# A two-layer encoder on one core: exponentials ordered behind a copy, five unread products, and one subtraction ahead of the masks

## The reference

```python
for l in range(DEPTH):
    h = _rmsnorm(x, attn_norm_w[l])
    (g_qkv, g_z, g_b, g_a, d_q, d_k, d_v, c_q, c_k, c_v, gate_raw) = _split_cols(h @ w_in[l])
    y_a = _gdn_mixer(g_qkv, g_z, g_b, g_a, ...)      # gated delta rule, both directions
    y_b = _diff_mixer(d_q, d_k, d_v, ...)            # differential attention, 4 heads
    y_c = _gqa_mixer(c_q, c_k, c_v, ...)             # grouped-query attention, 8 heads
    merged = (gates[:, :, 0] * (y_a @ w_branch_a[l]) + gates[:, :, 1] * (y_b @ w_branch_b[l])
              + gates[:, :, 2] * (y_c @ w_branch_c[l]))
    x = x + merged @ w_out[l]
    x = x + _hier_moe(_rmsnorm(x, ffn_norm_w[l]), ...)   # 32 experts, top 2 within the top group
return _rmsnorm(x, final_norm_w)
```

## Time and profile before

| | |
|---|---|
| median of 3 runs | 1574.89 us |
| the runs | 1576.79, 1574.89, 1573.20 us |
| the profiled execution | 1572.78 us |
| its span, first to last instruction | 1570.5 us |
| mean granted clock of TensorE | 0.94 of full speed |
| busy: PE, PEld, DVE, ACT, POOL | 1288.2, 998.3, 681.1, 445.7, 121.0 us |
| DMA | 491 MB, mean 313 GB/s |

### The profile page before, as it was taken

How to read it: one execution, slowest core, us unless ns; L and a number is a source line. 1 busy time by engine, 2 the same in 40 slices (tenths; PEclk the granted TensorE clock), 3 DMA queues, 4 the chain that set the end, 5 groups by cost and what they waited for, 6 DMA issues and landing times. The chain is left out here.

```text
span 1570.5 us, 42304 instructions
## 1 busy us (share of the span) xinstructions
PE 1288.2 (82%) x17356; PEld 998.3 (64%) x17357; DVE 681.1 (43%) x1682; ACT 445.7 (28%) x902; POOL 121.0 (8%) x110
## 2 busy tenths in 40 slices
PE   7998899998886667668799988999898867666665
PEld 6787687776655455446578876787666645445443
DVE  6667856663221221122286777666522321121222
ACT  4456645551000000000145565554400000000000
POOL 2002630000000000000020044200000000000000
PEclk9999999999998988889899999999999988888988
DMA  9521425599999999999974122446999999999996
GB/s 345 203 78 54 135 103 184 212 387 413 424 426 426 427 428 427 428 427 427 410 258 161 55 83 98 174 166 259 387 385 411 426 427 426 428 428 428 427 427 286
DMA packets 81207, 491.05 MB, mean 313 GB/s; under 512 B 13374, under 2 KB 15958, under 8 KB 53718
## 3 DMA queue, kind: packets, MB, share of 16 engines
q1 hardware_dynamic: 81110, 489.68, 76.9%
HBM read 488.61 MB, written 1.05 MB: 312 GB/s over the span
## 5 line engine op out<-in xcount | busy, mean ns | idle before, releaser
L2111 PE MATMUL ps<-ring,arena 128*32 128x128 f32 x5504 | 207.7, 311 | 122.5 <-DMA ring<-in_expert_w_gate_dram 78.4
L2111 PEld LDWEIGHTS ps<-ring,arena 128*32 128x32 f32 x5504 | 179.0, 125 | 161.9 <-DMA ring<-in_expert_w_gate_dram 80.1
L2210 ACT ACTIVATE arena<-ps 128x128 f32<-128x128 f32 x66 | 18.3, 277 | 498.2 <-PE ps L2111 498.2
L2111 PE MATMUL ps<-arena 128*32 128x128 f32 x2688 | 103.9, 313 | 60.0 <-DMA arena<-in_expert_w_gate_dram 42.7
L2316 DVE COPY arena<-ps 128x256 f32<-128x256 f32 x68 | 28.9, 425 | 276.0 <-PE ps L2077 275.9
L2111 PEld LDWEIGHTS ps<-arena 128*32 128x32 f32 x2688 | 89.2, 127 | 79.9 <-DMA arena<-in_expert_w_gate_dram 49.0
L506 POOL TENSOR_TENSOR small<-small,cst 128x8 f32<-128x8 f32 (+1 forms) x21 | 27.7, 1317 | 1193.4 <-DVE small L782 444.5
L1849 DVE TENSOR_TENSOR w_low<-ring,w_high 128x512 fp32r<-128x512 f32 x126 | 85.8, 706 | 52.0 <-ACT w_high L1773 52.0
L2138 PE MATMUL ps<-ring,arena 128*32 128x256 f32 x1376 | 88.7, 389 | 20.7 <-DMA ring<-in_expert_w_down_dram 19.6
L2375 DVE TENSOR_TENSOR arena<-ps,arena 128x128 f32<-128x128 f32 x66 | 25.0, 379 | 181.5 <-ACT arena L2210 181.5
L2212 ACT ACTIVATE arena<-ps 128x256 f32<-128x256 f32 x66 | 25.3, 383 | 275.3 <-PE ps L2138 275.3
(11 more groups left out here) (375 smaller groups left out, 2416.7 us busy)
## 6 DMA issues: line engine op xcount, KB each, us to landing
ring<-in_expert_w_up_dram SPq DMA_DIRECT2D x42, 2048.0 KB, 40.6
ring<-in_expert_w_gate_dram SPq DMA_DIRECT2D x42, 2048.0 KB, 40.4
ring<-in_w_in_dram SPq DMA_DIRECT2D x28, 2048.0 KB, 8.6
ring<-in_expert_w_down_dram SPq DMA_DIRECT2D x44, 1024.0 KB, 39.4
ring<-in_expert_w_down_dram SPq DMA_DIRECT2D x20, 2048.0 KB, 41.9
arena<-in_expert_w_up_dram SPq DMA_DIRECT2D x20, 2048.0 KB, 41.6
arena<-in_expert_w_gate_dram SPq DMA_DIRECT2D x20, 2048.0 KB, 40.3
arena<-in_expert_w_down_dram SPq DMA_DIRECT2D x20, 2048.0 KB, 42.0
```

Source lines behind the costliest of these rows:

```text
L2111: ins = pe.matmul(bank_b[32 * g:32 * g + 32, u * P:(u + 1) * P], xg[:, c], spare[u][:, c, g] if from_spare else w[:, u, c, g], start=(c == ...
```

## The change

```diff
@@ PE, attention block
                 for s in range(STEPS):
                     if s == STEPS - 1:
                         decay_sums()
+                        for n in range(2):
+                            pe.matmul(ps[1][:, :], ident, dv[:, n], start=True, stop=True)
                     if s < LATE:
@@ ACT, attention block
                         act.activation(probsT[:, f % 2].rearrange("p k q -> p (k q)"), ps[4][:, :], ACT.Copy).then_inc(c_pT, 1)
+                        if m == 0 and 4 <= s < STEPS - 1:
+                            exps(s + 1)
                         if s == LATE and m == 0:
                             silu(2)
                     if s >= LATE:
                         emptied(pieces[s])
-                    if s + 2 < STEPS:
+                    if s + 2 < 5:
                         exps(s + 2)
@@ PE, recurrence
                 for q in range(4):
                     dense(q)
+                for n in range(3):
+                    pe.matmul(ps[1 + n % 2][:, :], ident, QT[:, 0:2], start=True, stop=True)
@@ POOL, recurrence
                 pool.memset(XBD, 0.0).then_inc(e_zero, 1)
-                for q in range(3):
+                for q in range(4):
                     early_low(q)
                 for G in range(4):
                     d, t = divmod(G, 2)
                     pool.wait_ge(e_e, G + 1)
                     pool.tensor_tensor(INT[:, G], E[:, G], all_heads(cum[d]), ALU.mult).then_inc(e_m, 1)
                 pool.memset(LTO, 0.0).then_inc(e_zero, 1)
-                early_low(3)
                 pool.memset(DIm, 0.0).then_inc(e_zero, 1)
```

## The result

| | before | change |
|---|---|---|
| executions beside each other | 6 | 6 |
| median | 1573.59 us | 1561.86 us |
| range | 1570.47 to 1576.79 us | 1559.47 to 1563.77 us, and one of 6689.76 us that was disturbed and is left out of the ratio (the median counts it; without it, 1561.03) |
| ratio to before | | 0.9928, 95% interval 0.9903 to 0.9952 |
| profiled execution, span | 1572.78, 1570.5 us | 1560.38, 1558.1 us |

A second set of the same kernel gave 0.9922.

The account below looks back on a forecast made before the run. Taken as bound by attention and opening latency chains ahead of a DMA-saturated expert stage. Order -2.8, POOL +0.6, clock falls -1.6 and -2.5 sum to -6.3 us: median 1574.9 to 1568.6, range 1565.5 to 1573.0.

Parts of the forecast that it names:

- the likeliest case: Whole kernel: the order gains, POOL's move costs a little, both clock falls go; -6.3 us to 1568.6, chance 0.52.
- Order of exponentials: Attention steps 4 to 6: exponentials behind the first copy let the second copy start 1.41 us earlier; -2.8 us over two layers.
- C: Rival: DVE, not ACT, bounds attention steps 4 to 6, so only the clock gains; -3.5 us to 1571.4, chance 0.06.
- D: Rival: exponentials between a step's two copies hold back the second copy in attention; +7.2 us to 1582.1, chance 0.05.
- Unread products at 0: Attention's last tile and recurrence's opening: two and three unread products fit in TensorE's waits, costing 0 at full clock.
- POOL's move: Recurrence's opening: fourth low half ahead of the masks costs +0.3 us per layer, +0.6 for two.
- Falls of the clock: Layer 1's attention tail and layer 0's recurrence opening: both low-clock stretches go; -1.6 and -2.5 us.
- A: Rival: the order gains, but a clock fall stays or comes at another thin place; -4.3 us to 1570.6, chance 0.24.
- B: Rival: unread products and denser order do not hold the clock; -2.2 us to 1572.7, chance 0.13.
- a microsecond saved in a chain moves the dense stage, the issues and the end with it: All later stages in either layer: starts and end shift by exactly what the attention and opening chains save.
- F: Experiments' theory: added instructions move where pieces of TensorE's program must arrive, and with them expert-stage gaps and falls; 4 to 5 us.
- S: Experiments' theory: an earlier arrival alone changes how expert-stage transfers fall; some 4 us beyond the order's own -2.7.

Follow-up runs that it names:

- order_only: Only ACT's order of exponentials and copies in attention changed, against the kernel before: median 1568.22 us, ratio 0.9955.
- no_unread: The change without its five unread products (ACT's order and POOL's low half only), against the kernel before: median 1568.45 us, ratio 0.9975.
- no_unread_pad: The change without its five unread products, plus ten unread 8-column products at the very start, against the kernel before: 1566.36 us, ratio 0.9953.
- three_ol: ACT's order, POOL's low half and only the opening's three unread products, against the kernel before: 1563.98 us, ratio 0.9929.
- two_ol: ACT's order, POOL's low half and only attention's two unread products, against the kernel before: 1564.35 us, ratio 0.9932.
- both padded ones: The whole change plus ten or thirty unread 8-column products at the very start, against the kernel before: ratios 0.9926 and 0.9992.
- unread_only: Only the two and the three unread products added to the kernel before, without order or low half: 1573.79 us, ratio 0.9990.
- low_only: Only POOL's fourth low half moved ahead of the masks, against the kernel before: 1574.12 us, ratio 0.9991.
- pad_sixty_four: The kernel before plus 64 unread products of 32 weight columns at the start (256 instructions): 1576.50 us, ratio 1.0023, attention starting 3.72 us late.
- change_pad_thirty: The whole change plus thirty unread 8-column products at the very start, against the kernel before: 1571.72 us, ratio 0.9992, attention starting 9.35 us later than in the change.

## Why the prediction was wrong

The direction was right and the mechanisms of the likeliest case were as well; the size was too small by 5 to 6 us.

- **Order of exponentials, -1.4 per layer:** measured -1.35, along the chain named. C fell, since the recurrence started 1.35 us earlier, and D, since the second copy was earlier, not later.
- **Unread products at 0:** right in both places. Attention takes 76.89 with them and 76.90 without (order_only, layer 1); the levels start at 14.70 with them and 14.72 without (no_unread). The cover in the opening came to 1.04 us, 0.8 forecast.
- **POOL's move, +0.6:** wrong by all of it; +0.02 per layer alone. The levels start 0.24 us behind the fifth low half, as the prediction read for before, and that one ends when it did (14.5 us after the block's start) in either order. The prediction had this in hand ("the same instructions stand ahead of it in either order") and charged 0.3 per layer on top. The worth of the move is the cover that it gives the three products: without it they stick out by 1.1 to 2.7 us.
- **Falls of the clock, -1.6 and -2.5:** both went, and the profile gives -1.63 and -2.53. The second number is right by luck in part: about 1.0 of it was the gap of missing instructions at 177.41, which the prediction took for the clock's. Over all traces: attention with the order and without the two products has 0 to 2.80 us over 76.89, 1.1 on average of eight, with a fall in the tail of five (order_only, no_unread, no_unread_pad, three_ol); with the two, none of ten has any (both profiles of the change, two_ol and both padded ones). Openings without the three products average 1.4 over 36.8 (sixteen, eleven with a fall), with them and the low half 0.3 (ten, none with a fall). Gaps of missing instructions make up 0.4 of the first and nearly all of the second, so the clock's part is 1.0. That is 2 x 1.1 + 2 x 1.0 = 4.2 us where 4.1 were priced; the near equality is luck too, since the price was taken from the two falls of one execution. Rivals A and B fell: in these ten and ten no fall of the clock stands in the tail or the opening. Only unread_only, without order and low half, had falls beside the products (921.8 and 949.1 us). The Trainium skill ("TensorE: Matmul & The Clock Gate", section "Why this matters for your kernels") lays such losses to long idle gaps; here 1.80 us of idle had a fall behind it (order_only), and 3.64 us had none (low_only).
- **The step that failed: "a microsecond saved in a chain moves the dense stage, the issues and the end with it", and nothing else changes.** It holds for the stages between (-0.05, +0.09, -0.28), but the expert stage was taken as a fixed length since DMA is saturated there. Its head isn't: PE runs out of instructions, falls to the lower clock and, as I read the DMA share of 0.93, frees slots late; to 340 MB it takes between 76.6 and 81.7 us from the stage's start. The term that the sum put at nothing measured -4.19 us in the profile, and another -1.39 at layer 0's experts. The first fits what the medians have over the touched stages; the second did not come again and was scatter.

How far is the cause of the 4.2 us in the head settled?

**Shown:** the first gap stands at a place counted in instructions (121, 113, 109 and 101 products for 0, 16, 24 and 40 instructions more), and it lasts until 1.3 to 1.5 us after its piece of the program has landed. In the eleven traces with a gap at this break, the piece's transfer started between 0.99 and 4.72 us after the start of the burst, and the gaps were 0.23 to 3.58 us. Each of the six gaps of over 3.3 us had a fall of the clock starting within 2 us of its end, and of the five shorter ones that of pad_sixty_four alone. Of the 14 traces, the five with a gap up to 0.62 us or none have heads of 76.6 to 77.3, the nine with 2.0 to 3.6 us have 77.5 to 81.7; by falls in the first 45 us, the seven without have 76.6 to 78.7 and the seven with have 77.5 to 81.7.

**Against the simple forms of F and S:** heads are short wherever order and low half stand together (76.6 to 78.7, eight traces) and longer elsewhere (78.6 to 81.7, six), whatever the count: no_unread has before's own count, and both padded forms of the change kept its time. Nor does the time of arrival decide by itself: low_only and no_unread reach the experts at 1120.90 and 1120.88 us and take 80.5 and 77.0, and change_pad_thirty arrives later than before (1125.63 against 1122.66) and takes 76.7. For F remain the 4 us that ten early products gave to before, and the whole piece that gave nothing.

**Open:** why the piece comes earlier in the traces with order and low half, and so what makes the head shorter. A trace is one execution, and no run changed the time of arrival alone. That 12 us of medians are 7 in the touched stages and about 5 behind them is the sum of what the traces show, not a proof for the 5.

## What to carry to other kernels

A few products that nobody reads, put where TensorE waits and some other chain is due later anyway, kept its clock here at the price of nothing; count the cover first (how long TensorE would wait there in any case), and move whatever else stands in their way (here POOL's low half), since alone they gave 0. Where an order edit frees PE, look at which wait it makes longer, for the clock can fall there. Price the stages behind an edit too: a stage with a saturated DMA can still change its length at its head, here by up to 5 us. Look there, and in short chains, for idle time marked "issue" that ends behind a transfer of instructions; it is easily booked to the clock. A control with the same number of instructions elsewhere tells the place of an edit from its count: it did so here (no_unread_pad).

## What the runs showed of the hardware

- TensorE's instructions came in 16,384-byte transfers of some 256 instructions (one more transfer, and the break back at its place, for 256 instructions more). In bursts of short products beside weight transfers TensorE ran dry for up to 3.58 us (marked "issue"), at a place given by the count, until 1.2 to 1.6 us after the transfer's end (83 of 85 gaps). It did so in the opening of the recurrence too, for up to 2.53 us.
- Forty unread instructions at the program's start changed the time by a ratio of 0.9972 (0.9958 to 0.9986); 256 did not, once the 3.7 us of later start are taken off.
- An 8-column product of float32 took 0.22 us per pass at the start of the program with 128 columns of weights (60 in 12.97 us, two passes each), and 0.055 with 32 (128 in 7.00 us).
- A DVE copy of 32x128 beside a POOL subtraction took 1.22 us, its fellows 0.22.
- Instruction for instruction equal layers of one execution differed by up to 3.9 us in the opening without unread products (order_only; 2.5 of it missing instructions), and by 0.03 to 0.7 us with them in the five profiles that also have the low half.
